# Writing the middle attention heads as loops of the instruction streams instead of in full: a hybrid decoder layer on one core

## The reference

```python
h  = rmsnorm(x)
z  = h @ w_in                    # q | k | v | forget-logit | rnn-x | rnn-gate
A  = forget_attend(q, k, v)      # 8 heads of 64, logits + sums of log f, softmax
R  = rg_lru(conv4(rnn-x)) * gelu(rnn-gate)
x  = x + concat(rmsnorm(A), rmsnorm(R)) @ w_out
x  = x + (gelu(conv3(g)) * val) @ w_ffn_down      # g | val = rmsnorm(x) @ w_ffn_up
y  = rmsnorm(x)
# samples: k_past = cache_k[page_table], v_past = cache_v[page_table]; 32 pages of 128 positions each
```

## Time and profile before

| what | value |
|---|---|
| median of 3 runs | 3229.61 us (3229.58 to 3232.55) |
| the profiled execution, its own time | 3229.58 us |
| its span | 3227.8 us |
| instructions recorded | 45185 |
| PE busy / PEld busy | 92% / 81% of the span |
| DVE, ACT, POOL busy | 44%, 23%, 37% |
| HBM traffic | 130 GB/s over the span |

### The profile page before, as it was taken

How to read it: one execution, slowest core, us unless ns; L and a number is a source line. 1 busy time by engine, 2 the same in 40 slices (tenths; PEclk the granted TensorE clock), 3 DMA queues, 4 the chain that set the end, 5 groups by cost and what they waited for, 6 DMA issues and landing times. The chain is left out here.

```text
span 3227.8 us, 45185 instructions
## 1 busy us (share of the span) xinstructions
PE 2984.7 (92%) x15701; PEld 2603.7 (81%) x15701; DVE 1424.1 (44%) x1921; ACT 756.6 (23%) x1534; POOL 1206.1 (37%) x577
## 2 busy tenths in 40 slices
PE   4999989786799888988999999999999999999998
PEld 4899878643355444547999999999999998999998
DVE  5312434377676666615135444554455443212221
ACT  7000323321233322334011000000000003443342
POOL 1111101136766667605773222222222223454443
PEclk9999999967799899998999999999999999999999
DMA  7212333336777888545461111111111114555553
GB/s 224 76 67 89 109 102 104 99 111 213 237 237 235 243 251 247 181 131 165 137 185 59 45 43 53 52 41 45 46 53 46 47 50 168 198 182 175 180 195 114
DMA packets 249037, 422.52 MB, mean 131 GB/s; under 512 B 44694, under 2 KB 152419, under 8 KB 244371
## 3 DMA queue, kind: packets, MB, share of 16 engines
q1 hardware_dynamic: 167986, 322.58, 31.4%
q10 hardware_dynamic: 80616, 97.07, 8.9%
q0 software_dynamic: 288, 1.05, 0.1%
HBM read 337.21 MB, written 83.46 MB: 130 GB/s over the span
## 5 line engine op out<-in xcount | busy, mean ns | idle before, releaser
L2561 PE MATMUL PS<-MH,VS 128*128 128x416 f32 (+1 forms) x4000 | 1080.5, 351 | 2.3 <-issue 2.2
L2561 PEld LDWEIGHTS PS<-MH,VS 128*128 128x128 f32 x4000 | 749.4, 188 | 12.5 <-issue 3.9
L2561 PE MATMUL PS<-ML,VS 128*128 128x416 f32 (+1 forms) x2000 | 699.8, 350 | 0.0
L2561 PEld LDWEIGHTS PS<-ML,VS 128*128 128x128 f32 x2000 | 376.1, 188 | 2.6 <-issue 0.8
L1071 POOL TENSOR_TENSOR DL<-DR,DH 128x1408 fp32r<-128x1408 f32 x80 | 258.5, 3231 | 287.5 <-ACT DH L1496 287.4
L924 POOL TENSOR_TENSOR prod<-Kpg,qb 128x1024 f32<-128x1024 f32 x118 | 279.3, 2367 | 152.1 <-DMA Kpg<-in_cache_k 75.8
L2445 PE MATMUL PS<-PT,VA 128*65 128x416 f32 (+16 forms) x816 | 332.6, 492 | 3.8 <-ACT PT L1359 3.2
L2649 PE MATMUL PS<-GH,DH 128*128 128x416 f32 (+1 forms) x880 | 315.7, 359 | 14.9 <-DVE GL L2157 7.5
L1000 POOL CAST VS<-VR 128x1024 fp32r<-128x1024 f32 x52 | 62.9, 1209 | 689.2 <-PE PS L2561 687.6
L2651 PE MATMUL PS<-GH,DL 128*128 128x416 f32 (+1 forms) x880 | 311.1, 354 | 0.0
L2650 PE MATMUL PS<-GL,DH 128*128 128x416 f32 (+1 forms) x880 | 309.8, 352 | 0.0
(11 more groups left out here) (287 smaller groups left out, 4459.5 us busy)
## 6 DMA issues: line engine op xcount, KB each, us to landing
Kpg<-in_cache_k SPq DMA_DIRECT2D x256, 256.0 KB, 4.5
Vpg<-in_cache_v SPq DMA_DIRECT2D x256, 256.0 KB, 4.3
DR<-in_w_down SPq DMA_DIRECT2D x80, 704.0 KB, 4.1
gT<-GO ACTq DMA_DIRECT2D x110, 208.0 KB, 2.0
VR<-in_w_up SPq DMA_DIRECT2D x44, 512.0 KB, 3.3
GRb<-gT SPq DMA_DIRECT2D x31, 416.0 KB, 5.3
WR<-in_w_stream SPq DMA_DIRECT2D x21, 512.0 KB, 3.4
GRa<-gT SPq DMA_DIRECT2D x24, 416.0 KB, 5.5
```

Source lines behind the costliest of these rows:

```text
L2561: mm = e.matmul(PS[:, j, 0:full(j)], w[:, u, k], x[:, k, j * BW:j * BW + full(j)], start=(k == 0 and q == 0), stop=(k == KC - 1 and q == 2))
```

## The change

On each of the five engines the outer loop over the middle heads becomes a loop of the instruction stream. Its body is two heads (the inner loop `v` stays written out, since the two use different buffers). PE, ACT and DVE make three turns, SP and POOL two. The head number `i` in `sync_head`, `pool_head`, `act_head`, `dve_head` and `pe_head` is then a register's value. The order of the work, the buffers, the tiles and the semaphores are as before.

```diff
@@ sync
-            for ii in range(2):
+            with e.Fori(0, 2) as ii:
                 for v in range(2):
                     sync_head(2 * ii + 1 + v, 1 - v, load_order(False, False), 2)
             sync_head(5, 1, load_order(False, False), 2)
@@ scalar
             act_head(0, 0, PLANS[0])
-            for ii in range(3):
+            with e.Fori(0, 3) as ii:
                 for v in range(2):
                     act_head(2 * ii + 1 + v, 1 - v, PLANS[1])
```

## The result

The changed kernel takes 3253.06 us (median of 5 runs, 3247.44 to 3260.01), the kernel before 3229.61: the ratio is 1.0073, with a 95% interval of 1.0059 to 1.0086, so 19 to 28 us slower. The forecast was 3260 in a range of 3236 to 3290. The profiled execution of the changed kernel took 3262.64 us, 9.6 more than its median. That is so with each kernel here in which PE stalls at a new branch (e1_pe_only 16, e6_slot 9), while the others stay within 5 of theirs, so the sizes of such stalls in the profiles are probably at the upper end of what the timed runs had. I take sizes from the timed runs where there are any.

The account below looks back on a forecast made before the run. The prediction took PE as the bound and SP's issue time as the second. PE's branches 18, SP's register steps 10 and the other engines' steps 2 made 30 us on 3229.6: 3260 us, range 3236 to 3290.

Parts of the forecast that it names:

- the likeliest case: The forecast itself, PE's branches and SP's lag both costing time: 3260 us, chance 0.66.
- Step 1: PE's two branches back, after heads 2 and 4: idle gap and slower clock, 9.2 us each, 18 for two.
- Step 2: Branches of ACT, DVE, POOL and SP: covered, costing nothing; up to 7 us for two with PE's gap gone.
- Step 3: SP's computed waits and addresses in heads 1 to 4 delay value pages: 2.5 us a head, 10 us.
- Step 4: Register steps in the heads: 0.3 us a head on PE, 2 us for six; ACT, DVE and POOL 0.
- Step 5: Written-out instructions go away, but the loop's code is fetched again in the same amount: 0 us.
- Branches alone: Rival: SP's lag is swallowed by the DMAs queued ahead of the pages; 3250 us, chance 0.10.
- PE's stream becomes the bound: Rival: PE's register steps in six heads don't hide, 39 us more; 3298 us, chance 0.08.
- No difference: Rival: body stays in place or queue covers the gap, SP's lag swallowed; 2 us at most, 3231 us, chance 0.12.
- Faster: Rival: body stays in place, later turns load no code, half the gaps ahead of `scores` go; 3215 us, chance 0.04.

Follow-up runs that it names:

- e1_pe_only: The kernel before with the new loop on PE alone, the other four engines keeping known numbers: 3247.24 us, +17.8.
- e6_slot: The changed kernel with PE's loop body placed at the start of a block of code, no hint: 3242.14 us, +15.0 over the kernel before.
- e10: The kernel before with head numbers computed in registers on PE alone, in one pass with no branch taken: 3228.01 us, +3.0.
- e8: The kernel before with the new loop on ACT and DVE alone: 3232.2 us, +5.1 by medians, 1.6 by the ratio.
- e2: The kernel before with the loops on SP, POOL, ACT and DVE, PE keeping its heads written out: 3237.11 us, +7.7.
- e3: The kernel before with the new loop on SP alone: 3231.06 us, +1.6.
- e11: The kernel before without SP's run-time bounds test of the page numbers: 3205.06 us, -19.9.
- e9: The changed kernel with hinted branches on all five engines and PE's loop body at a block's start: 3234.78 us, +9.8 over the kernel before.
- e4: The kernel before with head numbers from registers on all five engines (not DVE's heads 5 and 6), no branch taken: 3238.75 us, +9.3.
- e5: The changed kernel with a prefetch hint for the branch back on all five engines: 3239.17 us, +12.1 over the kernel before.

## Why the prediction came out as it did

The time fell in the range, 7 us below the forecast, and the likeliest case was the right one. Its terms were less good than its sum: SP's steps were too large, the other engines' too small, and in the branches two errors of opposite sign nearly cancelled. That the sum came within 7 us is in part luck.

**Step 1, PE's branches.** Place, number and kind were right: two stalls, at the starts of heads 3 and 5 and not at head 1, with the clock at its lower level behind them, and the code loaded again. The net gap was forecast at 6.7 us and is 7.4 and 7.0. The clock was forecast at 2.5 us a branch, from a stretch of 14 us in which PE was mostly idle; it took some 8, since the slow stretch lasts longer than that row could show. What the step left out altogether is what is late next: the value pages used the stall, and their waits fell by 11 to 13 us, of which some 5 went to longer waits for the maxima. With 14.8 us measured (e1 less e10, to within some 7) against 18, the term came out near, by two errors of opposite sign, and not all of what the profile shows at a branch is found in the time. The body was estimated at 1,890 instructions, with 180 waits a head; the trace has 107 more register steps a head on PE, and 1,803 and 1,805 records from one of its branches to the next. The body of the recurrent stage, taken as 1,688 with nothing else counted, has 1,796: the two are of one size. By the earlier trace rows I argued from the number of instructions alone, and the size did point the right way. e6 shows that the number does not decide: the same body stays in place when it begins at a block's start.

**Step 2, the other engines' branches.** Right for ACT, whose branch takes 2.5 to 3.5 us where 3.5 was given; DVE and POOL take 0.3. Beneath PE's stall nothing of it is seen, and with that stall gone it is 2.7 us a branch, 5.5 for two, where "up to 7" was given; in time, e8 has 1.6 to 5.1 us with its register steps. That it goes unseen in the changed kernel is seen in e1 and e2, whose sum (25.5) is no less than 23.5, but only to within some 8 us.

**Step 3, SP's register steps.** This is the term that was too large: 10 us, measured 1.6 (0 to 6.5). The lag itself was nearly right. A head of SP got 56 more instructions in e3 (29 of them ahead of waits, the rest mostly for addresses), where some 50 steps were counted, and in the changed kernel's timeline the eight fetches of a set of pages take

```profile
1106.94 0.55 SPq L567 DMA_DIRECT2D Qst<-qT  x1
...
1113.73 4.77 SPq L603 DMA_DIRECT2D Vpg<-in_cache_v  x8
```

0.45 us more than the earlier trace rows, and the stretch from the first operand to them 0.56 more: about 1.8 for 32 fetches and 1.1 for the ten operands. The six other reads of the page table are not in this; the trace has 0.06 to 0.09 us from one such instruction to the next, so that 56 come to some 4 us a head, against 4.6 in the prediction. What failed is the share that reaches PE. The prediction let two thirds of what delays a value page reach PE, 2.5 us of the 4.6. But e11 takes 16 us a head off SP, and heads 1 to 7 get 1.9 us a head shorter, an eighth. An eighth of 4 us for four heads is 2 us, which agrees with e3. (That adding and taking away have the same share is assumed here.)

The sign that I had named for this step, gaps ahead of the value pages longer by 2 to 4 us in heads 1 to 4, is there, and misleads: the four heads wait 23.8 us in the changed kernel (9.7, 8.3, 1.7, 4.1) and 11.7 before. But e3, with SP's loop alone, has 23.8 as well, and its heads 1 to 4 take 363.5 us where the kernel before takes 361.4; and e10, which leaves SP as it was, waits 18.5 us (4.7, 5.0, 4.4, 4.4) and takes 356.4. A gap is a cost only if the head gets longer.

But the reading behind the step, that SP's issue time is the second bound, was right, and worth nearly as much as the whole change cost: 20 us. It had been there in the earlier trace rows (SP works through four fifths of heads 2 to 5), and I looked at it only for what the change adds.

**Step 4, register steps on PE, ACT, DVE and POOL.** Too small: 2 us, against some 10 for all steps, of which SP's are 1.6. PE's own 107 a head, nearly all hidden, as the step said, cost 3.0 (by the interval, -1 to 8). Some 5 us are left for DVE, ACT and POOL (and for the loops' ends), which the step put at zero because they are idle a third of the time or more. They are in chains with PE, though, and a step ahead of an instruction that PE waits for delays PE however idle the engine is on the whole. This is argued: no run had the steps of these three alone, and e8, which has ACT's and DVE's with their branches, gives 1.6 to 5.1 us for both. How the 5 us are shared stays open.

**Step 5, what goes away.** Right: nothing. That code already in place would save loads was true only with the hint, and saved no time by itself: e9 with 65 loads costs what e4 does with 79.

**The rivals.** *Branches alone* (3250) was nearer to the time than the forecast, and for SP it was right; it is wrong in that steps cost some 10 us with no branch taken. *PE's stream becomes the bound* falls with e10. *No difference* falls for the plain loop. The Trainium skill ("Runtime: NRT & Kernel Launch", section on instruction fetch mechanics) gives PE room for 2,048 instructions; a body of some 1,805 did stay in place with the hint and, from its second turn, when it began at a block's start, so the size agrees with the loads counted here (65 and 74). That a plain loop of this size stays there too does not follow, and the 84 loads contradict it. *Faster* falls as well: half of the 29.0 us ahead of `scores` should have gone if late code caused them. With the body loaded once, as in e5, the same row reads (heads 2 to 5)

```profile
PEld PS L2429 <- issue: 31.6, 62, 1.7
```

against 29.0 before: they are not late code.

What stays open: why the profiled executions of kernels with a stall of PE at a new branch run 9 to 16 us over their medians; which blocks the five extra loads fetch; what the end of a loop costs; and what in the placement decides. Only one placement was tried beside the changed kernel's own.

## What to carry to other kernels

A loop on TensorE costs not only the gap at the branch but the slow clock behind it, and pays back what others were late with: size it by the whole ledger of a head, and try the hint on the back edge first, since it took the stall away at both loops where it was tried. Before a change is made because of what it adds to a queue, ask what that queue does now that it needn't: here two instructions for each page number, in a queue that worked four fifths of the time, were worth 20 us, and the loop's stall 15. An engine's mean idle time doesn't make a step on it free when its results are waited for one by one.

## What the runs showed of the hardware

- A branch back on TensorE to a body of seven blocks of code (some 1,805 instructions) costs 4.1 to 5.9 us, one tile, and 2.0 to 2.2 us more; with the hint 0.5. In the recurrent stage (1,796 instructions) it is 9.0 and 0.5. A branch back of ACT takes 2.5 to 3.5 us until its next instruction, one of SP 2.9 to 3.8, of DVE and POOL 0.3.
- The hint keeps the body: 65 loads of code instead of 84. Placed at the start of a block, the body is loaded twice and then kept (74 loads), and the second piece of the gap is gone.
- After 7 us with next to no work, the clock is at 1.2 GHz for most of 24 us (0.59 and 0.60 on the mean), and 82 products take 21.9 us where 86 took 14.05. In e6, after a gap of 5.6 us, the 24 us behind it have 0.90.
- A run-time bounds test is two instructions a number on SyncE, 0.125 us each, and nothing in a profile's busy times shows it: only the gaps between its DMAs do.
